# A 2048-token prompt's input projection as one level of Strassen's algorithm

## The chip, the cores and the metric

The kernel runs on one core of a Trainium2 chip. A core has TensorE (matmuls, and weight loads beside them), VectorE, ScalarE, GpSimd and SyncE (SP), each with its own queue of instructions in program order, and 16 DMA engines that carry what SP, ScalarE and GpSimd issue. The metric is the device time of one launch in microseconds; less is better.

## The reference

One decoder step in fp32: a prompt of 2048 tokens and a sample of 8 x 8 new tokens, model width 1024. Both go through one projection into attention queries, keys and values, gates, and the inputs of a gated linear attention (GLA).

```python
h = rms_norm(x, ln_w)
proj = jnp.einsum('bsd,de->bse', h, w_in)          # w_in: 1024 x 8720
aq, ak, av, az, gq, gk, gv, gz, glr, mg_a, mg_b = jnp.split(proj, splits, axis=-1)
aq = partial_rope(aq.reshape(B, S, ATTN_HEADS, HEAD_DIM), pos) * (HEAD_DIM ** -0.5)
ak = partial_rope(ak.reshape(B, S, ATTN_HEADS, HEAD_DIM), pos)
# three groups of dilated windowed attention over prompt and sample, the GLA recurrence, then
ya = jnp.einsum('bsc,cd->bsd', o_attn * jax.nn.silu(az), w_attn_out)
yb = jnp.einsum('bsc,cd->bsd', o_gla * jax.nn.silu(gz), w_gla_out)
x + jnp.einsum('bsd,de->bse', jax.nn.sigmoid(mg_a) * ya + jax.nn.sigmoid(mg_b) * yb, w_out)
```

Outputs are both results, the last rows of keys and values, and the GLA states.

## The kernel before

The stages follow one another: the projection (`project`, slot by slot), then attention with the GLA recurrence (steps q of `attend` and `recur`), then the sample's attention and the output products (`finish`).

The projection works on halves of 1024 prompt tokens. The half's normalised tokens lie transposed on chip as `hT_hi` and `hT_lo`, the rounded value and the rest; the weights too (`whi`, `wlo`), so a product is three matmuls: high by high, high by low, low by high. `CHUNKS` orders each half into turns, one for each chunk of 512 columns (16 token-major chunks, GQK feature-major, and the narrow GLR). A turn has eight slots, one for each tile of 128 tokens, and in the first half a ninth for the sample's rows (`new`). A slot is eight contraction steps of three matmuls of 512 columns into one of two accumulator banks (`ACCS`); TensorE waits in `slot` until the bank is evacuated and, in a turn's first slot, for `w_lo`.

Beside it, for each slot: ScalarE evacuates the bank into `stage` (`evac`, L741, or L739 with a sigmoid for gates), VectorE applies rope to chunks 0 to 5 (`rope`, L975 to L979) or multiplies for SiLU (L958), and SP stores the tile to the DRAM tensor `tm` (`store`). The next chunk's weights come 1024 rows by 512 columns through `raw` (`load_pair`, L462); ScalarE rounds each slice times the norm weight (`split_hi`, L727), VectorE forms the rest (`split_lo`, L926). Token tiles are normalised one a slot, in the first turn of the first half and in its last turn for the second half: ScalarE squares (L699) and takes a root (L705), VectorE finishes (`stats`, L906 to L914), TensorE transposes (`transpose_x`, L1203), ScalarE rounds (L711) and VectorE subtracts (L920).

In the second half GpSimd loads cached keys (`ck`, L664) and rows of sample queries (`cq`, over the buffer `a_x`, ring of three, L676) for 216 items; VectorE multiplies the two (L987) and sums by head (L991) in `score`. GpSimd also copies windows of keys and values from `tm` to the outputs (`copy_window`, L655). At the end of the half, attention's first loads and the first of the sample's cached values (`load_v` of `finish`, into freed token and weight buffers) begin.

## Time and profile before

| | us |
|---|---|
| median of 3 runs | 2543.93 |
| lowest and highest | 2541.37, 2544.34 |
| profiled execution, its own time | 2544.25 |
| its span, first to last instruction | 2542.5 |

| engine | busy, us | share of the span |
|---|---|---|
| TensorE, matmuls | 2438.7 | 96% |
| VectorE | 1276.0 | 50% |
| ScalarE | 798.4 | 31% |
| GpSimd | 216.6 | 9% |

A line of the profile names an engine, a line of the kernel, an operation, and what is written out of what is read. A busy time is the sum of single durations; matmuls overlap in the pipeline, so the pace is read from counts in a stretch. Idle time before an instruction is put down to what released it.

### The profile page before, as it was taken

The page shows a single profiled execution, that of the slowest core. Times are in us where ns is not written, and L with a number is a line of the kernel's source. Part 1 is how long each engine was busy: PE and PEld are TensorE (multiplying, and loading weights), DVE is VectorE, ACT ScalarE, POOL GpSimd, SP SyncE. Part 2 cuts the span into 40 slices and gives each one's busy share as a digit, 9 for nine tenths or more (in the row PEclk, how much of TensorE's full clock was granted, in tenths as well). Part 3 has the DMA queues.
Part 4 walks back from the last instruction along what each step waited for, and adds up shares of the span by engine and source line. Part 5 has one row for each costly group of instructions (what it writes and reads, how often), then busy time and mean ns, then how long its engine had stood idle before and what let it go on. Part 6 is the DMA issues. An engine that isn't in the chain of part 4 may idle for free. (4 is left out here: it accounts for less than half of the span.)

```text
span 2542.5 us, 37016 instructions
## 1 busy us (share of the span) xinstructions
PE 2438.7 (96%) x13690; PEld 1978.7 (78%) x13690; DVE 1276.0 (50%) x2963; ACT 798.4 (31%) x1915; POOL 216.6 (9%) x383
## 2 busy tenths in 40 slices
PE   9999999999999999999999999788898987999998
PEld 7888878888888888888877888667777744888887
DVE  5321311211114565666546553677787865665663
ACT  5221222222224322222222221666666533222221
POOL 0000000000000112222233221000000000000000
PEclk9999999999999999999999999999999998999999
DMA  6332222222223457767799778654343369543441
GB/s 190 102 97 82 96 87 89 94 91 89 95 93 123 129 157 227 222 215 227 223 312 290 215 217 246 214 187 143 126 159 125 123 193 346 220 157 119 156 173 67
DMA packets 207137, 413.99 MB, mean 163 GB/s; under 512 B 32000, under 2 KB 52816, under 8 KB 204848
## 3 DMA queue, kind: packets, MB, share of 16 engines
q1 hardware_dynamic: 164928, 290.61, 34.5%
q0 software_dynamic: 29712, 95.06, 13.2%
q10 hardware_dynamic: 12320, 25.96, 2.7%
q8 instruction: 111, 1.82, 0.3%
q14 instruction: 66, 0.54, 0.1%
HBM read 310.48 MB, written 112.86 MB: 167 GB/s over the span
## 5 line engine op out<-in xcount | busy, mean ns | idle before, releaser
L1209 PE MATMUL b_acc<-b_whi,hT_hi 128*128 128x512 f32 x2048 | 799.8, 391 | 8.9 <-DVE b_wlo L926 4.5
L1211 PE MATMUL b_acc<-b_whi,hT_lo 128*128 128x512 f32 x2048 | 797.7, 389 | 0.0
L1210 PE MATMUL b_acc<-b_wlo,hT_hi 128*128 128x512 f32 x2048 | 797.6, 389 | 0.0
L1209 PEld LDWEIGHTS b_acc<-b_whi,hT_hi 128*128 128x128 f32 x2048 | 384.8, 188 | 91.2 <-DVE b_wlo L926 5.3
L1211 PEld LDWEIGHTS b_acc<-b_whi,hT_lo 128*128 128x128 f32 x2048 | 384.8, 188 | 80.3
L1210 PEld LDWEIGHTS b_acc<-b_wlo,hT_hi 128*128 128x128 f32 x2048 | 384.8, 188 | 79.2
L926 DVE SCALAR_TENSOR_TENSOR b_wlo<-b_raw,a_lnw,b_whi 128x512 fp32r<-128x512 f32 x268 | 193.3, 749 | 448.9 <-ACT b_whi L727 448.8
L741 ACT COPY b_stage<-b_acc 128x512 f32<-128x512 f32 (+2 forms) x198 | 115.9, 585 | 726.7 <-PE b_acc L1211 707.9
L758 ACT ACTIVATE c_sm<-c_sm,c_ends 128x256 f32<-128x256 f32 (+1 forms) x384 | 172.4, 451 | 73.7 <-DVE c_ends L1025 73.4
L739 ACT ACTIVATE b_stage<-b_acc 128x512 f32<-128x512 f32 x96 | 57.4, 598 | 425.6 <-PE b_acc L1211 425.6
L727 ACT ACTIVATE b_whi<-b_raw,a_lnw 128x512 fp32r<-128x512 f32 x268 | 186.1, 720 | 7.7 <-DMA b_raw<-in_w_in 4.3
L987 DVE TENSOR_TENSOR a_x<-a_x,b_ck 128x512 f32<-128x512 f32 (+1 forms) x216 | 147.8, 684 | 78.7 <-DMA a_x<-tm 78.6
L975 DVE TENSOR_TENSOR b_rc<-b_stage,b_cs 128x128 f32<-128x128 f32 (+1 forms) x102 | 29.7, 291 | 246.7 <-ACT b_stage L741 245.9
L676 POOL DMA_DIRECT2D a_x<-tm x216 | 118.8, 550 | 380.9 <-DVE sT L991 306.6
L1025 DVE CUSTOM_DVE_ANT_0 c_sm<-c_p_s,c_mask 128x256 f32<-128x256 f32 (+1 forms) x384 | 117.2, 361 | 43.5 <-PE c_p_s L1265 42.4
L991 DVE TENSOR_REDUCE sT<-a_x 128x8 f32<-128x512 f32 x192 | 131.7, 686 | 6.6
L1289 PE MATMUL c_p_o<-c_pT,c_v 128*64 128x128 f32 x1200 | 91.0, 290 | 27.2 <-ACT c_pT L788 27.1
L1976 PE MATMUL f_p_b<-w_wb_hi,f_bT_hi 128*128 128x512 f32 x256 | 102.6, 401 | 5.6 <-DVE f_bT_lo L2525 4.1
L1265 PE MATMUL c_p_s<-c_kT,c_qT 64*128 64x128 f32 x1200 | 93.9, 291 | 12.0 <-DVE c_ends L1025 12.0
L1977 PE MATMUL f_p_b<-w_wb_lo,f_bT_hi 128*128 128x512 f32 x256 | 100.8, 394 | 0.0
L1978 PE MATMUL f_p_b<-w_wb_hi,f_bT_lo 128*128 128x512 f32 x256 | 100.8, 394 | 0.0
L1265 PEld LDWEIGHTS c_p_s<-c_kT,c_qT 64*128 64x128 f32 x1200 | 77.1, 193 | 29.1 <-issue 28.1
(315 smaller groups left out, 3033.8 us busy)
## 6 DMA issues: line engine op xcount, KB each, us to landing
b_raw<-in_w_in SPq DMA_DIRECT2D x134, 512.0 KB, 4.3
tm<-b_stage SPq DMA_DIRECT2D x256, 256.0 KB, 2.3
a_x<-tm POOLq DMA_DIRECT2D x192, 256.0 KB, 4.8
b_ck<-in_cache_kv_w POOLq DMA_DIRECT2D x104, 256.0 KB, 4.9
c_qk<-tm SPq DMA_DIRECT2D x96, 256.0 KB, 3.5
f_m<-tm SPq DMA_DIRECT2D x16, 1024.0 KB, 5.8
og<-c_og ACTq DMA_DIRECT2D x48, 264.0 KB, 3.8
c_v<-tm SPq DMA_DIRECT2D x48, 256.0 KB, 4.5
```

The lines of the kernel that those rows point to most:

```text
L676: pool.dma_start(dst, src).then_inc(cq_in[m % CQ_RING], 16)
L727: nc.scalar.activation(whi[:, j % W_RING, :], raw_slice(j), ACT.Copy, scale=lnw[:, k:k + 1]).then_inc(w_hi, 1)
L741: nc.scalar.copy(out, src).then_inc(evacd, 1)
L758: last = nc.scalar.activation(y, y, ACT.Exp, bias=o[:, hh:hh + 1], scale=-1.0, accum_out=o[:, NH + hh:NH + hh + 1])
L926: V.scalar_tensor_tensor(out=wlo[:, j % W_RING, :], in0=raw_slice(j), scalar=lnw[:, k:k + 1], in1=whi[:, j % W_RING, :].bitcast(F32), op0= ...
L987: V.tensor_tensor(y, y, ck[0:r, u % CK_RING, :], ALU.mult).then_inc(multiplied, 1)
L991: V.tensor_reduce(out, y.rearrange("p (h e) -> p h e", h=NH), AX_X, ALU.add).then_inc(scored, 1)
L1025: last = V.tensor_tensor_reduce(out=sm[:, x.u % 4, h, lo:], in0=p_s[:, h, at + lo:at + 2 * P], in1=mask[:, lo:], scale=-HD ** -0.5, scalar ...
L1209: nc.tensor.matmul(out, stat_hi, mov_hi, start=(k == 0), stop=False)
L1210: nc.tensor.matmul(out, stat_hi, mov_lo, start=False, stop=False)
L1211: return nc.tensor.matmul(out, stat_lo, mov_hi, start=False, stop=(k == KC - 1))
L1265: last = nc.tensor.matmul(p_s[:, h, at:at + P], qT[r, x.i % 2, x.c, :], kT[r, n % KEPT, x.c, :], start=True, stop=True)
```

## The change

The projection of a half is arranged as 2 x 2 blocks: even and odd token tiles, upper and lower half of the contraction, and two chunks of columns. A turn of `CHUNKS` is now a pair of chunks (GQK is split into its two 256-column parts; GLR stays as it was) and has seven phases, P1 to Q3, each one product of a token form (`A_OF`) and a weight block or form over half the contraction (`KH` = 4 steps). A slot is one phase of one pair of tiles. The sample's rows are multiplied in four of the phases with plain blocks.

The token forms S1 to S4 are made by VectorE (`stage`, from the transposed tiles); a tile's share of them is spread over the slots of A1, A2, B1 and B2. Norm weights are now multiplied into the tokens. The weight forms T1 to T4 are made once, in the first half, by DMAs that GpSimd issues: copies and accumulating DMAs between `w_in` and a new DRAM tensor `t`, one turn ahead. SP loads block by block (ring of three), ScalarE rounds (ring of two), VectorE subtracts. The seven products are combined as they leave the accumulators, now six banks: ScalarE copies phase P1, VectorE adds the others in buffers `v`, `u` and `st`, from which the four results of a pair are stored. Gates are taken from these buffers by ScalarE afterwards.

`score` keeps its two VectorE instructions; its ring of query rows has four buffers. Window copies are issued once their chunk is stored. Attention's loads and the recurrence's constants wait for other events, since the buffers lie elsewhere (`project_over` waits for all products, stores, rope and scores), and the sample's cached values go to 13 places of one 1 MB transfer each.

The core of the diff:

```diff
-CHUNKS = ((7, 1, 4, 6, 0, 3, GQK, GLR, 9, 10, 11, 12, 13, 14, 15, 8, 2, 5),
-          (8, 2, 5, 7, 1, 4, 6, 0, 3, GQK, GLR, 9, 10, 11, 12, 13, 14, 15))
-W_RING, RAW_RING, STAGES, ACCS, X_RING, CQ_RING, CK_RING, IDLE = 12, 4, 4, 2, 3, 3, 3, (6, 2)
-Slot = namedtuple("Slot", "s half c chunk t kind last")
-Turn = namedtuple("Turn", "half chunk first last")
+CHUNKS = ((0, 6), (3, 7), (1, 8), (4, 9), (GQK,), (GLR,), (2, 12), (5, 13), (10, 14), (11, 15))
+N_TURN, NPAIRS, NFORM, KH = len(CHUNKS), TPH // 2, 7, KC // 2
+HI_RING, LO_RING, ACCS, X_RING, CQ_RING, CK_RING, IDLE = 2, 3, 6, 2, 4, 3, (6, 2)
+
+
+P1, P2, P6, P7, Q4, Q5, Q3 = range(NFORM)
+A11, A12, S2, S3, S1, S4, A22 = range(NFORM)
+A_OF = (A11, A12, S2, S3, A22, S1, S4)
+B11, B21, T2, T3, T4, T1, B22 = range(NFORM)
+T_ROW = {T1: 0, T3: 1, T2: 2, T4: 3}
+N_T = N_TURN - 1
...
+                for phase in range(NFORM):
+                    first = len(slots)
+                    units = [(kind, p) for p in range(NPAIRS if kind == "tm" else 2)]
+                    if half == 0 and phase in (P1, P2, Q5, Q3):
+                        units.append(("new", 0))
+                    for what, p in units:
+                        if (what, phase) == ("new", Q5):
+                            low_rows = chains
+                        chain = low_rows if (what, phase) == ("new", Q3) else chains
+                        if chain == chains:
+                            chains += 1
+                        slots.append(Slot(len(slots), half, len(turns), what, phase, p, len(blocks), chain))
+                    blocks.append((len(turns), phase, first, len(slots) - 1))
...
+    act_of = {"tm": {P1: 1}, "fm": {P1: 1}, "glr": {None: 1}, "new": {P1: 1, P2: 1, Q3: 1, None: 1}}
+    dve_of = {"tm": {P2: 1, P6: 1, P7: 1, Q4: 1, Q5: 2, Q3: 1}, "fm": {P2: 1, P6: 1, P7: 1, Q4: 1, Q5: 2, Q3: 1}, "glr": {},
+              "new": {P1: 1, P2: 2, Q3: 2, None: 2}}
...
+    NORM = [0, 2, 4, 6, NT, 1, 3, 5, 7] + [8, 10, 12, 14, 9, 11, 13, 15]
+    N_TILE = len(NORM)
+    odd_tile = lambda i: NORM[i] != NT and NORM[i] % 2 == 1
+    pair_of = lambda i: NORM[i] % TPH // 2
+    half_of = lambda i: NORM[i] // TPH if NORM[i] < NT else 0
+    turn_at = [-1, 0, 1, 2, 3, 5, 6, 7, 8] + [tail + n for n in (11, 13, 15, 17, 24, 26, 28, 30)]
+    stat_at = [max(-1, t - 1) for t in turn_at]
...
-    item_at = [begin + 3 + m * (NSLOT - 6 - begin - 3) // N_IT for m in range(N_IT)]
+    item_at = [begin + 4 + m * (NSLOT - 8 - begin - 4) // N_IT for m in range(N_IT)]
...
+                def load_w(b):
+                    turn, phase = turns[blocks[b][0]], blocks[b][1]
+                    if b >= LO_RING:
+                        sp.wait_ge(mm_done, blocks[b - LO_RING][3] + 1)
+                    if phase in T_ROW:
+                        sp.wait_ge(t_in, t_due(turn, phase))
+                        width = width_of(b)
+                        src = t_part(turn.n % N_TURN, phase, width).rearrange("(c p) e -> p c e", p=P)
...
+                def weight_sums(turn):
+                    (c1, width), (c2, _) = w_cols(turn, 0), w_cols(turn, 1)
+                    top, low = slice(0, D // 2), slice(D // 2, D)
+                    b11, b12 = WD[top, c1:c1 + width], WD[top, c2:c2 + width]
+                    b21, b22 = WD[low, c1:c1 + width], WD[low, c2:c2 + width]
+                    t1, t2, t3, t4 = [t_part(turn.n, form, width) for form in (T1, T2, T3, T4)]
+                    done = t_due(turn, T1) - 16 * T_DMAS
+                    pool.dma_start(t3, b22).then_inc(t_in, 16)
+                    pool.dma_start(t2, b11).then_inc(t_in, 16)
+                    pool.wait_ge(t_in, done + 32)
+                    pool.dma_start(t3, b12, accum_op=ALU.add, max_dma_last_dim=2048).then_inc(t_in, 16)
+                    pool.wait_ge(t_in, done + 48)
+                    pool.dma_start(t2, t3, accum_op=ALU.add, max_dma_last_dim=2048).then_inc(t_in, 16)
+                    pool.wait_ge(t_in, done + 64)
+                    pool.dma_start(t4, b21).then_inc(t_in, 16)
+                    pool.dma_start(t1, b11).then_inc(t_in, 16)
+                    pool.wait_ge(t_in, done + 96)
+                    pool.dma_start(t4, t2, accum_op=ALU.add, max_dma_last_dim=2048).then_inc(t_in, 16)
+                    pool.dma_start(t1, b12, accum_op=ALU.add, max_dma_last_dim=2048).then_inc(t_in, 16)
+                    pool.wait_ge(t_in, done + 128)
...
+                        if turn.n:
+                            pool.wait_ge(mm_done, turns[turn.n - 1].begin + 1)
+                        weight_sums(turn)
...
+                        nc.scalar.copy(whi[:, b % HI_RING, part, 0:w], w_raw[:, k, part, 0:w]).then_inc(w_hi, 1)
...
+                    group_free(act, x)
...
+                        nc.scalar.copy(vb[:, x.p, :], bank).then_inc(act_ev, 1)
...
+                    V.scalar_tensor_tensor(out=x, in0=x, scalar=m[2], in1=lnw_row[0:r, :], op0=ALU.mult, op1=ALU.mult
...
+                    elif what == "A1":
+                        dve.wait_ge(tr_done, i + 1)
+                        form_free(dve, i, Q5)
+                        dve.wait_ge(h_act, h_act_no[what, i])
+                        link(V.tensor_tensor(a_lo[:, A22, :, c], pt_part(1), hi(A22), ALU.subtract))
+                        link(V.tensor_tensor(raw(S3), hi(A11), pt_part(0), ALU.subtract))
+                        link(V.tensor_tensor(raw(S3), raw(S3), lo(A11), ALU.add))
+                        link(V.scalar_tensor_tensor(out=raw(S2), in0=raw(S3), scalar=-1.0, in1=pt_part(1), op0=ALU.mult,
+                                                    op1=ALU.subtract))
+                        link(V.tensor_tensor(raw(S1), raw(S2), hi(A11), ALU.add))
+                        V.tensor_tensor(raw(S1), raw(S1), lo(A11), ALU.add).then_inc(h_dve, 1)
+                    elif what == "A2":
+                        dve.wait_ge(h_act, h_act_no[what, i])
+                        V.tensor_tensor(a_lo[:, S2:S1 + 1, :, c], a_sum[:, S2:S1 + 1, :, c],
+                                        a_hi[:, S2:S1 + 1, :, c].bitcast(F32), ALU.subtract).then_inc(h_dve, 1)
+                    elif what == "B1":
+                        dve.wait_ge(h_dve, h_dve_no["A2", i])
+                        form_free(dve, i, Q3)
+                        link(V.tensor_tensor(raw(S4), hi(S2), lo(S2), ALU.add))
+                        link(V.tensor_tensor(raw(S4), raw(S4), hi(A12), ALU.add))
+                        V.tensor_tensor(raw(S4), raw(S4), lo(A12), ALU.add).then_inc(h_dve, 1)
+                    else:
+                        dve.wait_ge(h_act, h_act_no[what, i])
+                        V.tensor_tensor(a_lo[:, S4, :, c], raw(S4), hi(S4), ALU.subtract).then_inc(h_dve, 1)
...
+                    bank, v_, u_, st_ = acc[:, x.chain % ACCS, :], vb[:, x.p, :], ub[:, x.p, :], stb[:, x.p, :]
+                    if x.phase == P2:
+                        dve.wait_ge(act_ev, act_no[slot_at[x.turn, x.kind, P1, x.p]])
+                        V.tensor_tensor(st_, bank, v_, ALU.add).then_inc(dve_ev, 1)
+                    elif x.phase == P6:
+                        V.tensor_tensor(u_, bank, v_, ALU.add).then_inc(dve_ev, 1)
+                    elif x.phase == P7:
+                        dve.wait_ge(dve_ev, dve_no[slot_at[x.turn, x.kind, P6, x.p]])
+                        V.tensor_tensor(v_, bank, u_, ALU.add).then_inc(dve_ev, 1)
+                    elif x.phase == Q4:
+                        dve.wait_ge(dve_ev, dve_no[slot_at[x.turn, x.kind, P7, x.p]])
+                        first_stored(dve, x)
+                        V.tensor_tensor(st_, bank, v_, ALU.add).then_inc(dve_ev, 1)
+                    elif x.phase == Q5:
+                        V.tensor_tensor(v_, bank, v_, ALU.subtract).then_inc(dve_ev, 1)
+                        V.tensor_tensor(u_, bank, u_, ALU.subtract).then_inc(dve_ev, 1)
+                    else:
+                        dve.wait_ge(dve_ev, dve_no[slot_at[x.turn, x.kind, Q5, x.p]])
+                        V.tensor_tensor(u_, bank, u_, ALU.add).then_inc(dve_ev, 1)
...
+                    bank = acc[:, x.chain % ACCS, :]
+                    first, last = k == 0 and x.s in opens, k == KH - 1 and closer[x.chain] == x.s
+                    hi, lo = whi[:, x.block % HI_RING, k, :], wlo[:, x.block % LO_RING, k, :]
+                    f = A_OF[x.phase]
                     if x.kind == "tm":
-                        t = slice(x.t * P, (x.t + 1) * P)
-                        return product(out, k, hT_hi[:, k, t], hT_lo[:, k, t], whi[:, w, :], wlo[:, w, :])
+                        c = slice(x.p * P, x.p * P + P)
+                        return product(bank, first, last, a_hi[:, f, k, c], a_lo[:, f, k, c], hi, lo)
...
+                def chain_free(c):
+                    s = closer[c]
+                    x = slots[s]
+                    if x.kind == "tm" and s in silu_no:
+                        pe.wait_ge(silued, silu_no[s])
+                    elif x.kind == "glr" or x.kind != "new" and x.phase == P1:
+                        pe.wait_ge(act_ev, act_no[s])
+                    else:
+                        pe.wait_ge(dve_ev, dve_no[s])
...
-HV_TILES, HV_PAIRS, HV_ROWS = range(3, 7), range(7, 11), range(18, 25)
+BLOCK_ORDER, BLOCK_AGAIN = (0, 7, 1, 2, 3, 6, 4, 5), (0, 1, 4, 5, 2, 3, 6, 7)
+V_SLOTS, V_SEMS = 13, 9
...
```

## Rows read from the trace of the kernel before

**Rows 1.** The page: span, and busy time of each engine.
```profile
span 2542.5 us, 37016 instructions
PE 2438.7 (96%) x13690; PEld 1978.7 (78%) x13690; DVE 1276.0 (50%) x2963; ACT 798.4 (31%) x1915; POOL 216.6 (9%) x383
```
**Rows 2.** Busy time by stretch; columns in its first line, stretches in us.
```profile
core 0: us, PE busy (x) PEld busy (x) DVE busy (x) ACT busy (x) POOL busy (x), PEclk, DMA share, GB/s
300.00:600.00 300.00, 300.00 (x1328) 245.90 (x1327) 55.84 (x87) 69.82 (x115) 0.00 (x0) 1.00 0.29 91
...
12.00:838.00 826.00, 823.19 (x3695) 678.92 (x3696) 208.03 (x515) 216.13 (x363) 0.00 (x0) 1.00 0.31 99
838.00:1598.00 760.00, 753.54 (x3322) 620.07 (x3321) 430.17 (x782) 169.81 (x272) 192.52 (x351) 1.00 0.75 227
...
2060.00:2136.00 76.00, 61.43 (x369) 25.69 (x370) 36.84 (x98) 20.70 (x58) 3.16 (x6) 0.93 0.90 299
```
**Rows 3.** Instructions of lines 1209, 1216: min/median/max ns, first to last start.
```profile
L1209 PE MATMUL b_acc<-b_whi,hT_hi x2048: 387/389/632, 11.9 to 1597.6; 128*128 128x512 f32 x187
...
L1216 PE MATMUL b_acc<-b_wlo,hs x136: 388/389/393, 66.0 to 839.9; 128*128 128x512 f32 x136
```
**Rows 4.** TensorE's waits, 1300 to 1450 us: us in total, times, longest.
```profile
PE b_acc L1209 <- DVE b_stage L958: 3.7, 2, 2.0
PE b_acc L1209 <- DVE b_wlo L926: 2.7, 1, 2.7
```
**Rows 5.** VectorE's groups by line and shape, 0 to 1480 us.
```profile
L926 DVE SCALAR_TENSOR_TENSOR b_wlo<-b_raw,a_lnw,b_whi 128x512 fp32r<-128x512 f32 x254 | 183.2, 749 | 418.9 <-ACT b_whi L727 418.8
...
L991 DVE TENSOR_REDUCE sT<-a_x 128x8 f32<-128x512 f32 x167 | 114.6, 686 | 5.8
L987 DVE TENSOR_TENSOR a_x<-a_x,b_ck 128x512 f32<-128x512 f32 x167 | 114.5, 685 | 66.1 <-DMA a_x<-tm 66.0
...
L958 DVE TENSOR_TENSOR b_stage<-b_stage,b_acc 128x512 f32<-128x512 f32 x32 | 21.9, 686 | 85.1 <-ACT b_stage L739 85.1
...
L920 DVE TENSOR_TENSOR hT_lo<-a_pt,hT_hi 128x1024 fp32r<-128x1024 f32 x16 | 19.5, 1221 | 13.3 <-ACT hT_hi L711 13.2
...
L909 DVE RECIPROCAL a_ms<-a_ms 128x1 f32<-128x1 f32 x16 | 2.6, 164 | 5.3 <-ACT a_ms L705 5.3
...
L920 DVE TENSOR_TENSOR hs<-a_pt,hs 128x512 fp32r<-128x512 f32 x1 | 0.7, 692 | 3.3 <-ACT hs L711 3.3
```
**Rows 6.** VectorE in order of time, 835 to 845 us: start, duration, us.
```profile
836.45 0.29 DVE L975 TENSOR_TENSOR b_rc<-b_stage,b_cs 128x128 f32<-128x128 f32 x1 [2.01 <-ACT b_stage L741]
...
837.12 0.22 DVE L979 TENSOR_TENSOR b_stage<-b_rc,b_rs 128x64 f32<-128x64 f32 x1
...
839.80 2.73 DVE L926 SCALAR_TENSOR_TENSOR b_wlo<-b_raw,a_lnw,b_whi 128x512 fp32r<-128x512 f32 x4
```
**Rows 7.** DMA, 838 to 1598 us; second line: issues, KB each, us to landing.
```profile
DMA packets 78679, 172.29 MB, mean 227 GB/s; under 512 B 10448, under 2 KB 20368, under 8 KB 78634
...
a_x<-tm POOLq DMA_DIRECT2D x192, 256.0 KB, 4.8
```
**Rows 8.** DMA queues, 1264 to 1362 us: packets, MB, share of 16 engines.
```profile
q0 software_dynamic: 6373, 21.84, 74.1%
q1 hardware_dynamic: 4012, 7.47, 22.2%
```
**Rows 9.** Line 987's waits, whole span: us in total, times.
```profile
  DMA a_x<-tm: 78.6, 42
```
**Rows 10.** ScalarE's table loads on the sigmoid line, 12 to 1598 us.
```profile
L739 ACT ACT_TABLE_LOAD x2 | 2.6, 1283 | 0.0
```
**Rows 11.** Window copies, line 655, whole span: min/median/max of issue to landing.
```profile
DMA to landing us min/median/max: 5.5/9.4/12.4
```
**Rows 12.** The chain that ended last, 1550 us to the end: start, us, what.
```profile
2088.55 9.55 DMA e_v_hT_lo<-in_cache_kv_w
```

More of the change, by code:

```diff
@@ new lines, in project @@
+    NSLOT, NBLOCK, NCHAIN = len(slots), len(blocks), slots[-1].chain + 1
+    W = plan_projection(nc)
+    begin, last_turn = turns[N_TURN].begin, turns[-1]
+    tail = turns[N_TURN - 1].begin
+    opens = {x.s for x in slots if x.s == min(y.s for y in slots if y.chain == x.chain)}
+    closer = {}
+    for x in slots:
+        closer[x.chain] = x.s
+    first_of = {x.chain: x.s for x in slots if x.s in opens}
+    slot_at = {(x.turn, x.kind, x.phase, x.p): x.s for x in slots}
+    chunk_of = lambda x: turns[x.turn].second if x.phase in (Q5, Q3) else turns[x.turn].first
@@ new lines, in one, with rank_one @@
+                    w = width_of(x.block)
+                    rows = k + (KH if x.phase in (P2, Q3) else 0)
+                    return pair(bank[:, 0:w], first, last, hs[:, rows, :], hi[:, 0:w], lo[:, 0:w])
+                def rank_one(x, k):
+                    bank = acc[:, x.chain % ACCS, :]
+                    first, last = k == 0, k == KC - 1
+                    if x.kind == "new":
+                        return nc.tensor.matmul(bank[:, 0:2 * RANK], hs[:, k, :], wr[:, k, :], start=first, stop=last)
+                    f = ((A11, A12), (S1, A22))[x.p][k // KH]
+                    stat = wr2[:, k % KH, :] if x.p and k >= KH else wr[:, k, :]
+                    return pair(bank[0:2 * RANK, :], first, last, stat, a_hi[:, f, k % KH, :], a_lo[:, f, k % KH, :])
@@ L1740, in tail @@
                 load_vn(0)
-            if q == 1:
-                for k in range(STAGES):
-                    sp.wait_ge(over.stored[k], over.stores[k])
-                load_v(2)
         def load_lse():
```

995 lines of the change are left out of this document (544 added, 451 removed).

## The prediction, made before the changed kernel was run

> **What bounds the kernel now.** I read the page's busy shares first [rows 1]: TensorE is busy for 96% of the span, every other engine for half of it or less. The stage table [rows 2] then shows where that is so. The projection runs from 12 to 1598 us; in both its halves TensorE is busy over 99% of the time at a granted clock of 1.00 (2.4 GHz), and VectorE for 25% of the first half and 57% of the second. Behind it come attention, a sample stage with idle time and the output product, which the change leaves nearly alone. The view of one line's instructions gives the borders: the first product starts at 11.9 us, the last slot of the sample's rows, which closes the first half, ends near 840, and the last step of the last product begins at 1597.6 [rows 3]. TensorE's two largest waits in the second half come to 6.4 us [rows 4]. So the projection, 62% of the span, is TensorE issuing matmuls without a gap, and fewer matmuls are worth their full price until another engine becomes late.
>
> The price: 1328 matmuls in the 300 us from 300 to 600 [rows 2], 0.2259 us each. (The 390 ns in the groups of matmuls is the latency of one, not the pace.)
>
> **TensorE's part.** Before, each half does 17 wide chunks x 8 tiles x 8 contraction steps x 3 products = 3264 matmuls of 512 columns. After, a turn takes two chunks and does 7 phases x 4 token pairs x 4 steps x 3 = 336 where there were 384; 8 such turns and the feature-major one (168) make 2856. Two halves save 816 x 0.2259 = **184 us**. The sample's rows cost the same (272 matmuls before; 256, and 32 half as wide, after), the low rank too. A turn becomes 28 slots of 2.71 us, 75.9 us, and 83 in the first half with its four sample slots. The floors: first half 828 - 92 = 736 us, second 758 - 92 = 666 us.
>
> **What is added, by engine.**
>
> *VectorE, second half.* Evacuation moves from one ScalarE copy per chunk to seven VectorE additions per pair and turn: 8 x 28 + 14 = 238 at 0.685 us, which is what an addition out of b_acc takes [rows 5], 163 us. Weights: 63 blocks instead of 136 slices, but 4 x 512 wide and 7/4 as many elements. No row is that wide; the 512 and 1024 wide subtractions took 0.692 and 1.221 us [rows 5], so 2048 take 1.221 + 2 x 0.529 = 2.28, and 56 x 2.28 + 7 x 1.22 = 136 us. The scores stay two VectorE instructions an item, as they already were: 216 x (0.685 + 0.686) = 296 us [rows 5]; only their ring grows from 3 to 4. Rope, 48 tiles x 0.89 us from its first start to its last end [rows 6], is 43; the SiLU products 16 x 0.68 = 11; the last token forms 16 x 0.685 = 11. Sum **660 us** in 666. Neighbours that don't depend on each other overlap by some 0.07 us (four in 2.73 us, not 4 x 0.749 [rows 6]), which may give back 45; so VectorE needs 615 to 660 us, in order, each step behind a semaphore.
>
> *Transfers, second half.* Before, 172 MB at 227 GB/s kept the DMA engines 0.75 busy [rows 2, 7], that is 303 GB/s when full. The weights grow from 36 to 62 MB: 199 MB / 303 = 657 us. While the window copies ran they were already at 0.96 [rows 8]. Three resources thus stand within 7% of the 666 us that TensorE wants. A score waits for its DMA at the head of VectorE's queue, and behind it stand the additions that free the six accumulator banks and the weight split that TensorE needs three slots later. Before, scores waited 78.6 us so, in 42 waits [rows 9], and it cost nothing. With four buffers at 2.9 us an item a load has 8.6 us, against a median of 4.8 [rows 7]; I take 30 of those 78.6 us as exposed, and a few for alternation. **+34 us** over the floor, second half 700; bounds 0 (all hidden) and 92 (no faster than before).
>
> *The first turn.* VectorE's sum: 28 + 5 additions 23, weights 16, nine statistics at 2.9 (six small steps of some 0.16 [rows 5], their handoffs, then a scaling with two inputs, 0.749 + 0.529 = 1.28) 26, even tiles 5.6, odd tiles 4 x (6 + 4 operations of 0.685 and one 1536 wide of 1.75) 34, rope 8: 113 us, against TensorE's 83 + 9 transpositions of 1 us = 92. It is 21 late at least; with the chain ScalarE to VectorE to TensorE for each tile I take **+30** (up to 55 if the formed weights are late too), and **+2** for the row of norm weights at the start.
>
> *The last turn of the first half.* It now prepares the second half's tokens while it evacuates gates. Over the whole turn VectorE has about 96 us to TensorE's 91, but in its last 8 slots stand four tiles' statistics, sums and the double additions of phase Q5: 4 x (2.9 + 5.9 + 2.7) = 46 us in 22. TensorE can't run ahead, for it transposes each tile itself and waits for its scaling. 25 late. ScalarE changes from sigmoid to square root and back there: before, the sigmoid line loaded its table once a half, 1.28 us each [rows 10]; now roots at slots 10, 12, 23, 25, 27 and 29 alternate with gates, 12 loads, 15 us, and some of that stands in the same chain. **+35** (15 to 50). The Trainium skill ("ScalarE: Activation LUTs", Table sets: the hidden batching unit) says to group calls by table set, since functions of different sets reload the table. By that the term is the 35 taken; with the loads wholly hidden it would be 25 and the time 2461. The two loads of before, where no root stood among sigmoids, fit the rule.
>
> *The formed weights.* GpSimd issues, for each turn of the first half, four copies and four accumulating DMAs of 1 MB between DRAM tensors, in five steps, each waiting for the last; SP waits for the sums ahead of the loads of those blocks, and behind SP's wait stand all stores, and so the buffers that the additions need. One chain must take no longer than a turn. TensorE's turns leave room: chain 0 starts at once, chain n is needed some 45 us into turn n, 8.5 chains in 724 us; the limit is **85 us**. The trace has no accumulating DMA. The nearest row is the window copy, also DRAM to DRAM on this queue: 512 KB took 5.5 us at best, 12.4 at worst [rows 11], which at 303 GB/s is 3.8 us fixed and 3.5 per MB. Steps of 2, 1, 1, 2 and 2 MB then take 47 us if an accumulation costs as much as a copy, 60 if twice; at the worst row's rate, 21 us for 1 MB and 38 for 2, 156. In the same turn weights (7.3 MB) and stores (4.3 MB) take 38 us of the same engines; in the chain's fixed gaps some of it fits, so about 27 come on top: 74 and 87. Each us over 85 costs 7.5. I take the dearer of the two near ends in part, **+10** (0 up to 7.5 x (156 - 85) = 530, the latter far from the copies' median of 9.4). The Trainium skill ("Collectives: The Full Stack", The bandwidth ceiling: the fold count and why AG ≠ RS ≠ AR) states that an add in the DMA is dearer not for its arithmetic but for a second source read, which halves the rate. No run so far shows it; by that alone the chain would take the 87, the term would be 15 and the time 2476.
>
> *Rest.* The sample's value loads go to 13 slots of whole 1 MB transfers; before, the chain that ended last has 9.6 us of such a load [rows 12]. The recurrence's constants move behind all stores. -8 to +10, taken as 0.
>
> **Sum.** -184 + 2 + 30 + 35 + 10 + 34 = -73 us. The profiled execution took 2544.25 us, span 2542.5, the median of the runs is 2543.93: 2544.25 - 73 = **2471 us**.
>
> **Rivals.**
> 1. *The chain of sums binds.* An accumulation costs three or four copies, GpSimd falls a little further behind each turn, SP stands at the wait, stores and TensorE behind it. For it: an unpriced operation, in a half whose DMA engines would already be near 0.9 busy with it. Against: the copies' rate, and 0.31 busy before [rows 2]. It decides from 96 us a chain, where -83 + 7.5 x 11 = 0; at 105 us the time is 2544 - 83 + 150 = 2611. Slower.
> 2. *VectorE keeps up.* Overlap brings its second half to 615 us and the ring hides every landing; first and last turn cost only 20 and 15: -184 + 2 + 20 + 15 = -147, 2397 us. For it: TensorE hardly ever waited [rows 4]. Against: all margins are under 8%.
> 3. *Three full resources block one another.* DMA at 0.95 lands late, VectorE stands at scores, additions and banks follow, and the second half takes its old 758 us: -15, 2529 us, 2515 to 2560. For it: waits of TensorE on VectorE appear already under the window copies [rows 4, 8].
>
> **How the numbers follow.** Forecast 0.55 (2425 to 2515), rival 1 0.20, rival 2 0.13, rival 3 0.12. The range reaches to both outer cases: 2385 to 2610, with about 0.06 below and 0.12 above. A measurement of this kernel can tell 0.2%, 5 us. Faster: 0.55 + 0.13 + 0.04 of rival 3 = 0.72; same 0.04; slower 0.20 + 0.04 = 0.24.
>
> **What would show it.** TensorE: 816 fewer products, still at 0.226 us. Second half: VectorE over 90% busy, its additions released by nothing but its own queue, TensorE's waits naming VectorE; if they name the DMA of scores or of stores, rival 3. First half: SP's longest wait on a DMA into the sum tensor, repeated each turn, is rival 1; a single one in turn 0 is the forecast. The slots at the end of the first half take some 6 us each for eight slots, with table loads between. The forecast is wrong if an accumulation takes over twice a copy, if TensorE's granted clock falls in stalls (it was 0.93 in the sample stage with its waits [rows 2]), or if attention starts later by more than 10 us after the last product.

## The result, and the profile after

The changed kernel takes 2515.58 us (median of 4 runs, 2510.99 to 2523.27), the kernel before 2542.92 in the same series (2541.37 to 2544.34): a ratio of 0.9896, 95% interval 0.9865 to 0.9926. It is faster by 27 us, where 73 were forecast; the time lies in the whole range and just above the forecast's own one (2425 to 2515). The profiled execution took 2510.99 us, the fastest of the four and 33.3 less than the profiled one of before; the sums below are made on it.

The page after, its span, busy times, and the costliest group of instructions (busy us, mean ns | idle us before it, and what ended most of it):

```profile
span 2509.2 us, 35829 instructions
...
PE 2297.8 (92%) x12902; PEld 1849.8 (74%) x12902; DVE 1733.1 (69%) x3405; ACT 818.4 (33%) x1699; POOL 276.3 (11%) x455
...
L1466 PE MATMUL b_acc<-b_whi,a_hi 128*128 128x512 f32 x1792 | 711.6, 397 | 57.8 <-DVE b_wlo L1140 54.2
```

Against [rows 1] TensorE has lost 141 us of work, but the span only 33: TensorE went from 96% busy to 92%. The last line already names one cause: 54.2 us, over the whole span, in which products waited for the split of a weight block.

The borders of the halves, from the instructions of two lines (min/median/max ns, first to last start), and then busy times by stretch, columns as in [rows 2]:

```profile
L1466 PE MATMUL b_acc<-b_whi,a_hi x1792: 389/389/776, 19.1 to 1567.0; 128*128 128x512 f32 x200
...
L1473 PE MATMUL b_acc<-b_wlo,hs x144: 279/389/628, 44.6 to 853.3; 128*128 128x512 f32 x128, 128*128 128x256 f32 x16
```

```profile
12.00:144.00 132.00, 104.75 (x439) 83.66 (x438) 102.83 (x187) 44.38 (x59) 12.23 (x14) 0.90 0.89 241
144.00:440.00 296.00, 296.00 (x1323) 245.03 (x1322) 157.53 (x262) 62.31 (x55) 20.22 (x24) 1.00 0.76 212
460.00:470.00 10.00, 0.00 (x0) 0.00 (x0) 0.00 (x0) 0.00 (x0) 1.03 (x1) 0.57 0.64 108
470.00:480.00 10.00, 0.00 (x0) 0.00 (x0) 0.35 (x2) 0.00 (x0) 1.29 (x2) 0.50 0.83 284
480.00:490.00 10.00, 4.83 (x14) 3.87 (x15) 3.10 (x3) 6.33 (x7) 2.10 (x2) 0.56 0.96 237
...
724.70:853.70 129.00, 100.54 (x433) 82.22 (x433) 84.58 (x135) 63.99 (x79) 0.00 (x0) 0.88 0.38 124
...
855.00:1568.00 713.00, 674.69 (x2899) 547.91 (x2897) 621.32 (x963) 163.81 (x153) 191.36 (x351) 0.98 0.86 279
```

The first half runs from 19.1 to 853.5 us, 834 where 828 were before [rows 3]: it gained nothing. The second runs to 1567, 714 where 758 were. Three stretches of the first half show why: the first turn, up to about 144; 460 to 480, in which TensorE does nothing at all; and the last turn, 129 us from 724.7 on, whose 433 instructions are worth 98. Between them, from 144 to 440, TensorE is busy without a break, at 0.2237 us an instruction.

TensorE's waits from 12 to 855 us and, after the dots, from 855 to 1568 (us in total, times, longest):

```profile
PE a_pt L1460 <- DVE a_x L1089: 40.3, 11, 6.1
PE b_acc L1466 <- DVE b_wlo L1140: 26.1, 1, 26.1
PE a_pt L1460 <- DVE b_u L1089: 13.1, 4, 6.4
...
PE b_acc L1466 <- DVE b_wlo L1140: 32.6, 17, 4.4
```

There is one wait of 26.1 us in the first half and seventeen short ones in the second; the others of the first half belong to a chain in which transpositions (L1460) wait for VectorE's scaling of a token tile (L1089).

The prediction's terms against these borders:

| term | forecast | measured | read from |
|---|---|---|---|
| 816 products fewer | -184 | -184 | a wide turn at full pace takes 76.2 us (below), worked out were 75.9 |
| start | +2 | +7 | first product 19.1 for 11.9 |
| first turn | +30 | +35 | 126.8 us, from 19.1 to 145.9, less 92 |
| formed weights | +10 | +27 | 440 to 490: 102 instructions, worth 23 us |
| last turn, first half | +35 | +38 | 129.0 us, less 91 |
| second half | +34 | +48 | 714 - 666 |
| behind the projection | 0 | -3 | 942.2 us from the last product's start, 944.9 before |
| sum | -73 | -32 | 2512, measured 2511 |

Every cost came out dearer than forecast, and two of them, the formed weights by 17 us and the second half by 14, carry most of the miss. What the table can't tell is whether the causes were those forecast, and for these two they were not.

### The profile page after: what moved, and what is told of

Same layout as the page of the kernel before. It is cut to its first block and busy times, and to the rows that moved or that the text cites. A ratio compares the mean times of both kernels' runs of the same rounds, so it can differ in the third digit from the quotient of the medians.

```text
span 2509.2 us, 35829 instructions
## 1 busy us (share of the span) xinstructions
PE 2297.8 (92%) x12902; PEld 1849.8 (74%) x12902; DVE 1733.1 (69%) x3405; ACT 818.4 (33%) x1699; POOL 276.3 (11%) x455
## 5 line engine op out<-in xcount | busy, mean ns | idle before, releaser
L1466 PE MATMUL b_acc<-b_whi,a_hi 128*128 128x512 f32 x1792 | 711.6, 397 | 57.8 <-DVE b_wlo L1140 54.2
L1467 PE MATMUL b_acc<-b_wlo,a_hi 128*128 128x512 f32 x1792 | 705.9, 394 | 0.0
L1468 PE MATMUL b_acc<-b_whi,a_lo 128*128 128x512 f32 x1792 | 705.1, 393 | 0.0
L1466 PEld LDWEIGHTS b_acc<-b_whi,a_hi 128*128 128x128 f32 x1792 | 342.8, 191 | 137.5 <-issue 60.5
L900 ACT CAST b_whi<-b_w 128x2048 fp32r<-128x2048 f32 (+1 forms) x127 | 228.7, 1801 | 532.7 <-PE b_acc L1468 296.1
L1468 PEld LDWEIGHTS b_acc<-b_whi,a_lo 128*128 128x128 f32 x1792 | 341.5, 191 | 72.4
L1467 PEld LDWEIGHTS b_acc<-b_wlo,a_hi 128*128 128x128 f32 x1792 | 342.5, 191 | 70.3
L1140 DVE TENSOR_TENSOR b_wlo<-b_w,b_whi 128x2048 fp32r<-128x2048 f32 (+1 forms) x127 | 272.9, 2150 | 56.9 <-ACT b_whi L900 56.6
L1239 DVE TENSOR_TENSOR a_x<-a_x,b_ck 128x512 f32<-128x512 f32 (+1 forms) x216 | 147.8, 684 | 36.4 <-DMA a_x<-tm 35.9
L1583 PEld LDWEIGHTS c_p_o<-c_pT,c_v 128*64 128x64 f32 x1200 | 66.3, 141 | 40.2 <-ACT c_pT L972 30.5
L2234 PE MATMUL f_p_z<-w_wo_hi,f_mT_hi 128*128 128x512 f32 x240 | 94.8, 395 | 0.0
L919 ACT COPY b_v<-b_acc 128x512 f32<-128x512 f32 x68 | 39.6, 587 | 167.7 <-PE b_acc L1468 78.0
```

What stands on the lines that cost most here:

```text
L900: nc.scalar.copy(whi[:, b % HI_RING, part, 0:w], w_raw[:, k, part, 0:w]).then_inc(w_hi, 1)
L1140: V.tensor_tensor(wlo[:, k, part, 0:w], w_raw[:, k, part, 0:w], whi[:, b % HI_RING, part, 0:w].bitcast(F32), ALU.subtract).then_inc(w_lo, 1)
L1239: V.tensor_tensor(y, y, ck[0:r, u % CK_RING, :], ALU.mult).then_inc(multiplied, 1)
L1466: nc.tensor.matmul(out, stat_hi, mov_hi, start=first, stop=False)
L1467: nc.tensor.matmul(out, stat_hi, mov_lo, start=False, stop=False)
L1468: return nc.tensor.matmul(out, stat_lo, mov_hi, start=False, stop=last)
```

## The experiments

**1. The sums one turn earlier.** GpSimd starts the sums of turn n when turn n-1 begins. Its timeline (start, duration, what ended the idle time) shows that the sums for the chunks (2, 12) began at 442:

```profile
442.31 0.66 POOL L766 DMA_DIRECT2D t<-in_w_in  x1 [93.11 <-PE b_acc L1473]
...
461.79 1.03 POOL L771 DMA_DIRECT2D t<-t  x1 [8.45 <-DMA t<-in_w_in]
470.92 0.66 POOL L773 DMA_DIRECT2D t<-in_w_in  x1 [8.09 <-DMA t<-t]
...
498.53 0.66 POOL L766 DMA_DIRECT2D t<-in_w_in  x1 [12.97 <-DMA t<-in_w_in]
```

GpSimd had waited 93.11 us for TensorE, because the turn ahead is the low-rank one, which takes 8 us (437.9 to 446.1) and not a wide turn's 83. SP had come to the first load of a formed block already at 438. It stood there for 32.3 us, and ScalarE, behind it, for 33.8:

```profile
SPq L574 <- DMA t<-t: 32.3, 1, 32.3
...
ACT b_v L919 <- DMA gl<-b_st: 33.8, 1, 33.8
```

TensorE doesn't get as far as a formed block. It stops at 459 us, after the turn's first phase, for the plain block B21, which had landed at 438.6: the rounding of that block stands in ScalarE's queue behind the copies of phase P1, these wait for the stores of the turn before (`gl`), and those stand in SP's queue behind its wait for the sum. If the late start is the cause, a start one turn earlier removes the stall; if the sums are too slow as such, it comes back elsewhere.

```diff
-  pool.wait_ge(mm_done, turns[turn.n - 1].begin + 1)
+  pool.wait_ge(mm_done, turns[turn.n - (2 if turns[turn.n - 1].kind == "glr" else 1)].begin + 1)
```

> The sums for the turn behind the narrow low-rank turn are issued one turn sooner (after the start of the feature-major turn, not of the low-rank one). Theory A: in the changed kernel TensorE stands still from 457 to 483 us, and runs at half its clock for some us after, because the turn ahead of that one lasts 11 us where the others last 83, so the chain of five DMA steps starts too late. Then the stall goes, and the first half, which ended at 854 us, ends at 822 to 829; the whole falls by 25 to 32 us, to about 2485. Rival B: the DMA engines are full there, the chain only moves the lateness into the turn before; then the first half ends at 845 or later and the whole falls by under 10 us.

Measured: 2495.84 us (2486.38 to 2498.32), ratio 0.9808 (0.9783 to 0.9832). The first half ends 23 us earlier, 1 us later than the expected range, and the whole, by the medians 20 us down, falls short of the 25 expected. TensorE works through the stretch where it stood:

```profile
460.00:480.00 20.00, 18.31 (x74) 14.98 (x75) 13.45 (x31) 5.66 (x6) 2.33 (x3) 0.91 0.88 243
...
L1473 PE MATMUL b_acc<-b_wlo,hs x144: 279/389/628, 44.8 to 830.2; 128*128 128x512 f32 x128, 128*128 128x256 f32 x16
```

SP's wait on L574 is gone, and of TensorE's 26.1 us one wait of 3.9 is left in that turn. So it was the lead and not the pace of the chains. The second half, 713 us from 830 on, is untouched.

**2 and 3. What the second half waits for.** VectorE is 87% busy there, the DMA engines 86%. The first edit takes one of two VectorE instructions from each score and leaves all transfers; the second takes away all but the first four loads of the scores' queries and leaves VectorE its two.

```diff
-  V.tensor_tensor(y, y, ck[0:r, u % CK_RING, :], ALU.mult).then_inc(multiplied, 1)
-  dve.wait_ge(multiplied, m + 1)
```

> The multiplication of sample scores is left out (VectorE sums the query rows by head as they are): 216 instructions of 0.685 us, 148 us of VectorE in the second half; every transfer stays. The second half took 714 us (854 to 1568) where TensorE's matmuls alone need 666. Theory VectorE (its queue is the bound): VectorE falls to some 475 us busy, and the second half to 675 to 685. Theory DMA (full engines make weights and query rows land late): the second half stays at 700 or more, and TensorE still waits some 20 us or more for the weights' remainders.

```diff
-  pool.dma_start(dst, src).then_inc(cq_in[m % CQ_RING], 16)
+  if m < CQ_RING:
+      pool.dma_start(dst, src).then_inc(cq_in[m % CQ_RING], 16)
...
-  dve.wait_ge(cq_in[m % CQ_RING], 16 * (m // CQ_RING) + 16)
+  dve.wait_ge(cq_in[m % CQ_RING], 16)
...
-  V.tensor_tensor(y, y, ck[0:r, u % CK_RING, :], ALU.mult).then_inc(multiplied, 1)
+  V.tensor_tensor(y, y, ck[0:r, u % CK_RING, :], ALU.max).then_inc(multiplied, 1)
```

> The loads of query rows are left out but for the first four (212 of 216, 52 of the 199 MB that the second half moves), and the product is a maximum, so that values stay bounded; VectorE does as many instructions of the same size as before, without waiting for those rows. Theory VectorE: the second half stays at 700 to 712. Theory DMA: weights land in 5 us, not 9, TensorE's waits for the weights' remainders go from 28 to under 8 us, and the second half takes 675 to 690.

Measured: 2497.14 and 2473.11 us, one run each. The four runs of the changed kernel lie 12 us apart, so what a single run shows is read from the stretches of its profile and not from its total. The second half without the multiplications and TensorE's wait in it:

```profile
851.00:1555.00 704.00, 670.05 (x2906) 547.88 (x2905) 480.45 (x749) 164.53 (x153) 191.95 (x351) 0.98 0.88 282
...
PE b_acc L1464 <- DVE b_wlo L1140: 31.5, 9, 7.8
```

And without the queries' loads, its first turn and all behind it, TensorE's wait, and the landing of the weights' loads:

```profile
853.30:939.20 85.90, 78.92 (x338) 64.54 (x337) 79.46 (x129) 21.13 (x19) 4.55 (x8) 0.96 0.44 144
939.30:1522.00 582.70, 580.98 (x2568) 477.37 (x2566) 539.47 (x836) 143.84 (x134) 71.96 (x131) 1.00 0.69 229
...
PE b_acc L1467 <- DVE b_wlo L1141: 6.2, 3, 4.5
...
DMA to landing us min/median/max: 3.5/6.2/11.1
```

VectorE, relieved of 141 us, gave 10 us back; the DMA engines, relieved of over a quarter of their load (146 MB for 199, by the rows' GB/s), gave 45, more than either side had expected, with VectorE as busy as ever, 619 us in 669.

The loss has two places, though. These are the changed kernel's first turn in that half, its second, and all behind the first:

```profile
853.70:939.60 85.90, 78.96 (x338) 64.53 (x337) 79.47 (x129) 21.14 (x19) 16.13 (x29) 0.96 0.55 175
939.60:1015.80 76.20, 76.20 (x338) 63.10 (x337) 73.12 (x120) 15.54 (x11) 22.38 (x42) 1.00 0.84 278
...
939.60:1568.00 628.40, 597.03 (x2569) 484.45 (x2567) 542.89 (x837) 143.50 (x134) 175.24 (x323) 0.98 0.90 293
```

The first turn is 10 us longer than the second, with the queries' loads or without, at a DMA share of 0.55 or 0.44: there the last token forms are made (experiment 8 takes it to 76.7 us). Behind it the loads' removal gives the whole 46 us back, down to full pace, 0.2263 us an instruction. About 16 of the 46 are not waits but slower products, 597.0 us busy for 581.0, at a granted clock of 0.98 for 1.00. And of the 10 us that VectorE's relief gave, 6 stand in the first turn (80.1 us there).

TensorE's wait names VectorE's split of the weights (L1140) in all of them, but that is only the last link: ahead of it stands ScalarE's rounding (L900), and ahead of that the weights' load. In the changed kernel ScalarE's waits from 855 to 1568 us, and the landing of those loads (line 586), are

```profile
ACT b_whi L900 <- DMA b_w<-t: 123.1, 13, 21.7
...
ACT b_v L919 <- DMA tm<-b_u: 51.0, 12, 15.4
...
ACT b_whi L900 <- DMA b_w<-in_w_in: 35.2, 4, 11.8
...
DMA to landing us min/median/max: 3.9/8.9/21.9
```

A load may start when the block three before it is used up, and its rounding is due when the one two before it is: 10.8 us, four slots of 2.71. The rounding (1.9 us) and the split (2.3) follow, so a load that lands 6.6 us later than that, 17.5 after its issue, stops TensorE even if ScalarE and VectorE drop everything for it. Four of the sixty loads land so late (17.7 to 21.9 us); without the queries none takes over 11.1. They alone don't make the stalls: experiment 5 below leaves none of them and most of the waits. In the others smaller delays add up ahead of the split. Loads are issued up to 8 us after their buffer came free, behind stores on SP, and roundings stand behind ScalarE's copies of phase P1 (L919), which wait 51 us for stores to land. How much each of these adds wasn't taken apart.

**4. The last turn's table loads.** ScalarE's table loads from 700 to 870 us, ten of twelve (L928 and L932 have one each):

```profile
L862 ACT ACT_TABLE_LOAD x6 | 7.7, 1283 | 0.1
L935 ACT ACT_TABLE_LOAD x4 | 5.1, 1283 | 0.1
```

The edit puts a copy in place of the sigmoid, in the last turn of the first half.

```diff
-  nc.scalar.activation(sgn, nb[0:NS, :], ACT.Sigmoid).then_inc(gated, 1)
+  nc.scalar.activation(sgn, nb[0:NS, :], ACT.Copy if x.turn == N_TURN - 1 else ACT.Sigmoid).then_inc(gated, 1)
...
```

> The sigmoids of the first half's last turn are copies, so those gates are wrong; nothing else changes. ScalarE then needs no table loads between roots and sigmoids. TensorE lost about 30 us between 800 and 860 us waiting for scaled tiles. Theory table loads: the 12 loads go and the stretch is 10 to 15 us shorter. Rival, VectorE's chain alone: the stretch is under 5 us shorter, since the loads stand beside VectorE's longer work.

Measured: 2512.05 us, one run. One load is left of the twelve, and the first half ends at 847.6 instead of 853.3, 6 us earlier, between the two outcomes expected. Two of the 6 stand ahead of the last turn, which began at 722.7 for 724.7; the turn itself is 125.2 us long for 129.0. So the loads cost about 4 us, which the rival expected, and the rest of the last turn's 38 is something else.

**5 and 6. Fewer bytes in two other ways.** Removing the queries' loads also takes work from GpSimd's queue. So once the window copies are moved out of the second half, into attention, two for each tile of the recurrence (on top of the first edit), and once half of each weight block is left unloaded, and with it unrounded and unsplit.

```diff
-  if copies and item_at[min(m, N_IT - 1)] >= turns[N_TURN + turn_with(3 + 3 * copies[0][1] + copies[0][0], 0)].end + 6:
+  if False:
       copy_window(*copies.pop(0))
-  while copies:
-      copy_window(*copies.pop(0))
   for n in range(NT):
       pool.wait_ge(go_evacd, n + 1)
+      for _ in range(2):
+          if copies:
+              copy_window(*copies.pop(0))
```

> On top of the earlier sums (e1): the 28 window copies (11.5 MB between DRAM tensors) leave the second half of the projection; GpSimd issues two of them after each of its tiles of the recurrence, in the attention stage, whose DMA share was 0.48. Theory DMA (bytes in the second half make weights land late): 6% fewer bytes take the second half from 713 to 695 to 705, the attention stage grows by no more than 3 us, the whole is 2475 to 2486. Rival: the copies fitted in the gaps, the second half stays within 4 us of 713, and the whole with it at 2488 to 2498.

```diff
+  elif turn.half:
+      sp.dma_start(dst[:, 0:KH // 2, :], src[:, 0:KH // 2, :]).then_inc(w_in[b % LO_RING], 16)
...
```

> In the second half of the projection only the first half of each weight block is loaded, rounded and subtracted (the other half is left from earlier, so results there are wrong): 31 of 199 MB fewer, on SP's queue, not GpSimd's, and some 66 us of VectorE less; the matmuls stay. Theory DMA bytes: the second half, 714 us in the changed kernel, takes 670 to 685, as without query rows (669). Rival, that it was GpSimd's queue and its descriptors that mattered and not bytes: 700 or more.

Measured: 2472.71 us (2469.55 to 2475.83), ratio 0.9728 (0.9711 to 0.9744), and 2476.52, one run. The second half of the one, with TensorE's wait and the weights' landing in it, and of the other:

```profile
826.00:1522.00 696.00, 667.33 (x2904) 543.86 (x2903) 621.05 (x964) 164.24 (x153) 175.91 (x323) 0.99 0.84 268
...
PE b_acc L1467 <- DVE b_wlo L1141: 24.7, 12, 4.5
...
DMA to landing us min/median/max: 3.8/8.6/14.6
```

```profile
853.00:1525.00 672.00, 661.87 (x2905) 542.47 (x2904) 561.37 (x965) 115.41 (x153) 191.41 (x351) 0.99 0.81 251
```

The copies' removal gave 17 us with VectorE's 621 us in place, and attention took 4 of them back (946.0 us after the last product for 942.2). Half the weights gave 42, with GpSimd's queue as it was; this edit also takes 60 us from VectorE and 49 from ScalarE, and some 6 of the 42 stand in the first turn (80.2 us), where VectorE counts. Whichever bytes go, the second half gets shorter.

**7. Another queue for the weights.** Were it the order on SP's queue, with stores ahead of the weights, a queue of their own would help: ScalarE issues the second half's weight loads.

```diff
+  act.wait_ge(mm_done, blocks[b - LO_RING][3] + 1)
...
+  act.dma_start(w_raw[:, b % LO_RING, :, 0:width], src).then_inc(w_in[b % LO_RING], 16)
```

> In the second half the weight blocks are issued by ScalarE as soon as their buffer is free, no longer by SP behind stores that wait for VectorE. Same bytes. Theory order (loads are issued late in SP's queue): weights land earlier, the second half takes 690 to 702. Theory DMA (issue is early enough, landing is slow): it stays at 708 to 718, and the median from issue to landing stays at 8 us or more.

Measured: 2527.71 us, one run, the second half 730 us, 16 longer, which neither side had expected:

```profile
852.00:1582.00 730.00, 679.10 (x2904) 551.63 (x2903) 622.51 (x965) 165.49 (x153) 191.45 (x351) 0.97 0.85 273
...
PE b_acc L1483 <- DVE b_wlo L1157: 44.5, 16, 5.1
...
DMA to landing us min/median/max: 3.6/8.6/19.6
```

The loads are issued sooner, 0.7 us in the mean after their buffer is free for 1.9, and land hardly faster, after 8.6 us in the median for 8.9. So the order on SP's queue alone was not the cause. Why it became slower wasn't shown; ScalarE now waits for a free buffer ahead of its other work, which may delay the roundings themselves.

**8. VectorE's chain in the last turn.** The token sums of the second half's tiles, formed there and at the start of the second half, are made for one of a tile's 128 tokens only, on VectorE and in ScalarE's rounding of them.

```diff
+  if what in ("A2", "B2") and half_of(i):
+      c = slice(c.start, c.start + 1)
...
+  c = slice(full.start, full.start + 1) if what != "E" and half_of(i) else full
...
-  link(V.tensor_tensor(raw(S3), hi(A11), pt_part(0), ALU.subtract))
+  link(V.tensor_tensor(raw(S3), hi(A11), few(pt_part(0)), ALU.subtract))
...
```

> The token sums S1 to S4 of the second half's odd tiles are made for one of 128 tokens only (results of the second half are wrong): about 6 us of VectorE less for each of four tiles, nothing less for TensorE. In the changed kernel the first half ends at 853 us; TensorE lost some 30 us from 800 to 860. Theory VectorE's chain: the end comes 15 to 24 us earlier. Rival, the statistics' chain through ScalarE and back sets the pace: under 8 us earlier.

Measured: 2492.76 us, one run. The last product of the sample's rows starts at 837.1 us, 16 earlier, with the table loads still there. The last turn of the first half, the first of the second, and all behind it:

```profile
722.50:837.50 115.00, 98.94 (x433) 80.24 (x433) 70.67 (x137) 60.42 (x80) 0.00 (x0) 0.93 0.42 140
837.50:914.20 76.70, 76.45 (x337) 62.98 (x337) 67.35 (x124) 17.64 (x18) 15.71 (x28) 1.00 0.64 194
914.20:1549.80 635.60, 596.13 (x2568) 482.81 (x2567) 543.62 (x838) 143.26 (x134) 175.69 (x323) 0.98 0.90 290
```

The last turn is 115.0 us long for 129.0 (2 of the 16 stand ahead of it), so the token sums carry 14 of its 38 us and the table loads about 4; the other 20 (statistics, scaling, gates' additions) were not taken apart. The second half's first turn is 9 us shorter too, but the rest of that half is 7 us longer, 635.6 for 628.4, with every transfer still there: the 10 us of the first turn can't simply be taken off the second half's loss.

**9 and 10. Toward a better kernel.** On top of 1 and 5, the first eight of the sample's value loads move behind the projection; and on top of that the gate chunks (11, 15) trade places with (4, 9), so that no sigmoid stands in a half's last turn.

```diff
-  block_load_at.setdefault(form_over[n % NFORM], []).append(k)
+  block_load_at.setdefault(NSLOT + 10 + 5 * k, []).append(k)
```

> On top of e5 (earlier sums, copies later): the first eight loads of the sample's cached values (8 MB) leave the end of the projection's second half for the attention stage, one every five slots. Theory DMA: at the 1.0 to 1.5 us per MB that the runs so far gave, the second half falls from 696 to 684 to 690, and the attention stage, whose start no longer shares the engines with them, does not grow; the whole falls by 5 to 14 us, to 2459 to 2468. Rival: these loads came in the last turn only and hid; the whole stays within 4 us of 2473.

```diff
-CHUNKS = ((0, 6), (3, 7), (1, 8), (4, 9), (GQK,), (GLR,), (2, 12), (5, 13), (10, 14), (11, 15))
+CHUNKS = ((0, 6), (3, 7), (1, 8), (11, 15), (GQK,), (GLR,), (2, 12), (5, 13), (10, 14), (4, 9))
```

> On top of e9: the turns of chunks (4, 9) and (11, 15) change places, so that the first half's last turn has no sigmoid among the square roots (but rope, about 1 us of VectorE more). Theory: with copies in place of sigmoids (e4) the first half ended 6 us earlier; here 3 to 7 us off the whole against e9. Rival: the rope and the later store of chunk 4, which attention reads, take it back: within 3 us of e9.

Measured: 2461.36 us (2457.81 to 2464.47), ratio 0.9669 (0.9640 to 0.9697), and 2452.05 (2444.76 to 2454.90), ratio 0.9632 (0.9606 to 0.9659). The ninth is 11 us faster than the fifth by the medians. The profiles show 5 of them, and little where they were expected: the second half takes 694.0 us, 2 less, and the stages behind it 943.3, 3 less; where the rest went stays open. The tenth has one table load from 700 to 870 us instead of twelve,

```profile
L863 ACT ACT_TABLE_LOAD x1 | 1.3, 1283 | 0.0
```

and gains 9 us, 2 more than the most expected: 3 in the first half (which ends at 822.7), 4 in the second, 3 behind it. The order of the chunks touches all three; which of it is the loads' wasn't taken apart. It is the fastest kernel of the study, 3.7% faster than before.

## Why the prediction was half right

The gain from fewer products, the prices of the instructions and the cost of the two turns with token work were right. The net gain was 27 us and not 73 because two steps failed: the lead that the formed weights have, and the way in which full DMA engines cost time in the second half.

**TensorE's gain: right.** 816 products at 0.226 us are worth 184 us, and a wide turn at full pace takes 76.2 us where 75.9 were worked out. That the second half comes to 669 us without the queries' loads, against a floor of 666, is partly chance: the 10 us of its first turn are in it, and the floor had kept the 6.4 us that TensorE waited in the old half [rows 4].

**The prices of VectorE's instructions: right.** 2.28 us were worked out for the subtraction of 2048 columns from two rows of narrower ones, 0.685 for an addition out of b_acc. VectorE's groups, 855 to 1568 us:

```profile
L1140 DVE TENSOR_TENSOR b_wlo<-b_w,b_whi 128x2048 fp32r<-128x2048 f32 x55 | 125.7, 2285 | 22.8 <-ACT b_whi L900 22.6
...
L1189 DVE TENSOR_TENSOR b_u<-b_acc,b_v 128x512 f32<-128x512 f32 x34 | 23.1, 681 | 3.6 <-PE b_acc L1468 3.6
```

Its sum for the second half was 615 to 660 us, and 621 it is.

**The second half: the wrong mechanism, its size off by 14.** The step that failed: "A score waits for its DMA at the head of VectorE's queue, and behind it stand the additions that free the six accumulator banks and the weight split", priced at 30 us and meant as a cost of VectorE's queue. The scores do wait, 35.9 us in 32 waits. But experiment 2, which shortens that queue by 141 us, gives only 10, and 6 of these in the first turn. That the term came within 14 us is luck. What sets the stretch is the transfers, named in rival 3: from 172 MB [rows 7] to

```profile
DMA packets 89050, 198.84 MB, mean 279 GB/s; under 512 B 9830, under 2 KB 17766, under 8 KB 89009
```

with the bytes as forecast (199 MB), and a landing of 6.5 us for a score's query instead of 4.8 [rows 7]. The prediction compared 657 us of transfers with 666 of products and took what fits in the mean as fitting. It has no term for how late a single weight load or store lands at a share of 0.86: the weights' loads have 10.8 us until their rounding is due, and ScalarE stands for them 17 times, for 158 us. Nor has it one for the clock: that the granted clock falls in stalls it named only as a sign of being wrong, the sign came true, and slower products make some 16 us of the loss. By its own test, "TensorE's waits naming VectorE; if they name the DMA of scores or of stores, rival 3", the answer is neither: they name VectorE's split, and one step further up the DMA of the weights, which was not on the list. Rival 3 had the late landings, but another path (VectorE standing at the scores) and an excess of price: 92 over the floor for the 48 that came.

**The formed weights: the right worry, the wrong place.** The step that failed: "chain n is needed some 45 us into turn n", and with it the rule that "one chain must take no longer than a turn". As a mean the rule holds: of the chains whose end shows, the first took 66.9 us less 1.3 and the one above 498.5 less 442.3, 66 and 56 us against a limit of 85. But SP, which loads ahead, stood for the first sum of the chunks (2, 12) at 438 us, 8 before their turn began, and the chain may only start when the turn ahead begins, which here is the short low-rank one: it started at 442. The path from there was as the prediction had it, stores behind SP's wait and buffers behind the stores. The cost is 27 us, once; not in turn 0, and not repeated, so the mark set for it ("a single one in turn 0 is the forecast") pointed at the wrong turn. The low-rank turn stands in the list of chunks that the diff shows.

TensorE's granted clock goes with the stall: 0.57 and then 0.50, the lower of its two levels (1.2 of 2.4 GHz), after the engine stood still, and still 0.56 from 480 to 490 when the products are back, 1.00 after that.

What an accumulation costs was left between one copy and two. In the least disturbed chain, GpSimd's steps from 316 us, the wait for two copies of 1 MB (L769) and the waits for one accumulation of 1 MB each (L771, L773) are

```profile
322.73 1.04 POOL L769 DMA_DIRECT2D t<-in_w_in  x1 [5.47 <-DMA t<-in_w_in]
329.14 1.01 POOL L771 DMA_DIRECT2D t<-t  x1 [5.38 <-DMA t<-in_w_in]
337.87 0.66 POOL L773 DMA_DIRECT2D t<-in_w_in  x1 [7.71 <-DMA t<-t]
```

1 MB accumulated takes as long as 2 MB copied, or a little longer. That agrees with the rule of the Trainium skill ("Collectives: The Full Stack", The bandwidth ceiling: the fold count and why AG ≠ RS ≠ AR) that the prediction weighed, a second source read for each byte, though no run shows that the read is the reason; the time that it would have given, 2476, fails with the same step, since the pace of the chains was not what cost.

**The first and the last turn of the first half: right in size, the last one's parts not.** +30 and +35 were forecast, 35 and 38 measured. TensorE's waits on L1089 fit VectorE's chain as worked out; for the first turn no run tests it. In the last one 14 us went with the token sums (experiment 8). The table loads, 10 of the 35, came as counted, twelve at 1.283 us where roots and sigmoids alternate and one where they don't. The rule on table sets ("ScalarE: Activation LUTs" of the Trainium skill, Table sets: the hidden batching unit) thus agrees with the trace. Taking the loads away gives about 4 us, so the chain beside them costs more than the 25 forecast.

**The start: too small.** 2 us were forecast for the row of norm weights, 7 came. VectorE copies the row, TensorE transposes it and ScalarE copies it again, all ahead of the first tile's square on ScalarE (the second line), which before started at 4.5 us:

```profile
10.76 1.01 ACT L866 COPY sT<-a_pt 128x1024 f32<-128x1024 f32 x1 [8.53 <-PE a_pt L1448]
11.67 1.06 ACT L857 ACTIVATE a_junk<-a_x 128x1024 f32<-128x1024 f32 x1
```

**Of the rivals**, the first (a chain of sums that binds each turn) and the second (VectorE the only worry, and it keeps up) fell; the third, at about half its price, is the second half's loss. The sign held because all losses together, some 150 us, stayed below the 184.

## What to carry to other kernels

For each piece of work that is started ahead, take the shortest of the stages that are to cover it, not the mean, and the time at which the loading queue first stands for it, not that of its use: an 8 us stage in a list of 83 us ones cost 27 us, and one changed index gave 23 of them back. Where TensorE, VectorE and the DMA engines all stand near nine tenths, sums of busy time don't tell which one binds; ask how late one transfer lands against its own look-ahead, take load from one resource at a time, and compare turn by turn. And where the DMA engines bind a stage, move out the bytes that nobody waits for there: without the window copies the stage was 17 us shorter, and the one that took them 4 us longer.

## What the runs showed that was not expected

Landing times rose well before the DMA engines were full: a weight block's load took 6.2 us in the median at a share of 0.66, 8.9 at 0.86, and its worst 11.1 and 21.9. And an engine that waits names only its neighbour: nearly all of the second half's stalls stand on VectorE's line L1140, and removing over a fifth of VectorE's work there left 31.5 of 32.6 us of them.
